# Up projections of three MLPs: high and low parts of the activations moved side by side as 512 columns

## The chip, the cores and the metric

The kernel runs on one core of one Trainium2 chip. The metric is device microseconds (us) for one execution of the whole program, from its start to its end on that core; lower is better. The median of three executions of the kernel before is 1496.93 us.

## What is computed

Two blocks of a network follow each other on the same 256 tokens of 1024 features. The first block has a short convolution layer and an RWKV layer, the second a sparse attention layer and a forgetting attention layer. After each of the four comes an MLP with a hidden width of 4096 and a squared ReLU, and only these MLPs matter here:

```python
# first_block, DEPTH = 2
h = _modulate(_rmsnorm(x, norm_g[i, 1]), sh2, sc2)
x = x + gt2[:, None, :] * (jnp.square(jax.nn.relu(h @ mlp_w1[i])) @ mlp_w2[i])
# second_block, DEPTH = 2
def sq_relu_mlp(xn, w_up, w_down):
    return jnp.square(jax.nn.relu(xn @ w_up)) @ w_down
```

`h @ mlp_w1` and `xn @ w_up` are the up projections (1024 to 4096), the others the down projections. All inputs and outputs are float32.

## The kernel before, in words

**Numbers in two parts.** Each float32 matrix is split into a high part (rounded to the type fp32r) and a low part (the rest). A product is the sum of three: high by high, high weight by low activation, low weight by high activation. The helper `three` (lines 1949 to 1951) issues these three matmuls into one accumulating PSUM bank.

**Units.** Weights arrive in units of 1 MB. SP loads a unit into one of four `stage` buffers, once the unit four before it has been split (`lo_made`). ScalarE copies it into `w_hi` (line 775) and VectorE subtracts to make `w_lo` (line 1310), each in two halves of 128 x 1024 elements. `w_hi` and `w_lo` have two buffers each, so unit u + 2 is split after unit u is done (`unit_done`) and while unit u + 1 is being multiplied.

**An MLP** has four groups, and each group has four up units and four down units; the two kinds take turns by group. An up unit multiplies eight row tiles of `h` (index `kt`) by two blocks of 128 output features (index `m`): 8 x 2 x 3 = 48 matmuls, with the weights as the stationary operand and 256 tokens as the moving one (128x256). It writes one bank, `un[0]` or `un[1]` in turn; the block `m` is one half of the bank. A down unit (`wide_unit`, lines 1990 to 1992) is 24 matmuls of 512 columns into the four `acc` banks.

**Behind an up unit**, in this order: ScalarE takes the ReLU out of PSUM (`relu_b`, line 932); VectorE forms max(un, 0) x relu into `zf` (line 1496), waits for it to be finished and then frees the bank with an `engine_nop` (`un_free`); both engines then split the weights of unit u + 2; ScalarE copies `zf` to `z_hi` (line 920) and VectorE subtracts to `z_lo` (line 1390). After the last up unit of a group (`j` = 3) the order differs: first half of the weights, then `z_hi` and `z_lo`, then the second half. `z_hi` and `z_lo` are what the down units multiply.

**Around an MLP.** `stat_ps` and `misc` are the two other PSUM banks. They serve norms, transposes and rows that are broadcast: before the MLP of the RWKV layer (`m` = 1), `row_copy(3, stat_ps, misc)` on ScalarE reads both (lines 915 and 916), after ScalarE has made the `h` tiles and split weights. Before the MLPs of the attention layers (`m` = 2, 3) the tiles of `h` are read from `acc`, `stat_ps` and `misc`. In the first unit of an MLP, TensorE waits for each tile of `h_lo` in turn, and transposes further tiles in between. In the first group of `m` = 2 and 3, the norm's sums are worked out beside the up units (`both_rms` on VectorE and `both_roots` on ScalarE, at `j` = 2).

**Names of the change:** `h_hi` and `h_lo` (SBUF, eight tiles of 256 columns each, in regions of their own), `un`, `stat_ps`, `misc`, `relu_b`, the functions `mlp` of the three engines and `unit` of TensorE.

## Time and profile before

| | us |
|---|---|
| median of three executions | 1496.93 (1493.68 to 1499.69) |
| the profiled execution, as timed | 1501.27 |
| its span in the trace | 1499.5 |
| mean granted TensorE clock | 0.969 of 2.4 GHz |

| engine | busy us | share of the span |
|---|---|---|
| TensorE, matmul | 1426.8 | 95% |
| TensorE, weight load | 1252.1 | 84% |
| VectorE | 854.6 | 57% |
| ScalarE | 696.3 | 46% |
| GpSimd | 112.5 | 8% |

The costliest groups of instructions by summed busy time (the records of matmuls overlap, so their sums are larger than the time that they take on the engine):

| line, engine | what | count | busy us | mean ns |
|---|---|---|---|---|
| L1310 VectorE | `w_lo` from `stage` and `w_hi` | 378 | 454.2 | 1239 |
| L775 ScalarE | `w_hi` from `stage` | 378 | 379.8 | 1049 |
| L1949 to L1951 TensorE | `un` from `h` and weights, 256 columns | 3 x 1536 | 449.2, 439.7, 439.5 | 292, 286, 286 |
| L1990 to L1992 TensorE | `acc` from `z` and weights, 512 columns | 3 x 640 | 252.9, 249.5, 249.3 | 395, 390, 390 |
| L932 ScalarE | `relu` from `un` | 64 | 38.2 | 597 |
| L1496 VectorE | `zf` from `un` and `relu` | 64 | 44.2 | 691 |
| L1390 VectorE | `z_lo` | 68 | 46.6 | 685 |

How to read it: a matmul's record runs from its start to its modelled end, and the next one starts before that end. What a matmul costs in a dense stream is the distance from its start to the next start. The time of an up unit is the distance between two ReLUs that each waited for TensorE. The chain of waits puts 88% of the span on TensorE.

### The profile page before, as it was taken

How to read it: one execution, taken by the hardware profiler on the slowest of the kernel's cores; microseconds unless marked ns; L12 is line 12 of the kernel's file. 1: busy time of each engine (PE TensorE's matmuls, PEld its weight loads, DVE VectorE, ACT ScalarE, POOL GpSimd, SP SyncE). 2: the span in 40 equal slices, each digit the busy share in tenths (PEclk: the TensorE clock that was granted, in tenths of full speed). 3: DMA queues.
4: the chain of work that ended last, by engine and by line, in shares of the span. 5: the costliest groups of instructions: out<-in, count | busy, mean ns of one | idle time of the engine just before them, and what ended most of it. 6: DMA issues, size and time to landing. Idle time of an engine off the chain costs nothing.

```text
span 1499.5 us, 28573 instructions
## 1 busy us (share of the span) xinstructions
PE 1426.8 (95%) x12399; PEld 1252.1 (84%) x12399; DVE 854.6 (57%) x1320; ACT 696.3 (46%) x1192; POOL 112.5 (8%) x114
## 2 busy tenths in 40 slices
PE   4999999999899999988999998899999999999997
PEld 1987778878697899868988997689999899899986
DVE  1447634446657445556555658766555668665555
ACT  2434533334376322445444534655444557564443
POOL 0000000010100444410000001100000012000000
PEclk8999999999998999989999979999999999999999
DMA  9998699945334200014566533236556454365551
GB/s 359 382 323 300 240 361 302 309 149 169 88 117 152 72 4 3 3 38 171 189 196 191 162 116 110 85 103 207 183 183 197 144 169 136 119 211 178 190 194 56
DMA packets 177430, 257.17 MB, mean 172 GB/s; under 512 B 10425, under 2 KB 122361, under 8 KB 177305
## 3 DMA queue, kind: packets, MB, share of 16 engines
q1 hardware_dynamic: 177304, 255.35, 51.3%
q8 instruction: 98, 1.61, 0.5%
q14 instruction: 28, 0.22, 0.0%
HBM read 254.28 MB, written 1.05 MB: 170 GB/s over the span
## 4 chain that ended last, share of the span: by engine, by line
PE 88%; DVE 5%; ACT 3%; DMA 1%; issue 1%; SPq 1%; POOL 0%; DVEq 0%; ACTq 0%; POOLq 0%
PE un L1949 14%; PE un L1950 14%; PE un L1951 14%; PE acc L1990 10%; PE acc L1991 9%; PE acc L1992 9%; PE acc L2248 4%; PE misc L2100 3%; DMA ada_buf<-in_ada_w 1%; DVE w_lo L1310 1%; PE misc L2248 1%; PE un L2248 1%; PE stat_ps L2248 1%; PE acc L2242 1%; ACT w_hi L775 1%
## 5 line engine op out<-in xcount | busy, mean ns | idle before, releaser
L1310 DVE TENSOR_TENSOR w_lo<-stage,w_hi 128x1024 fp32r<-128x1024 f32 (+1 forms) x378 | 454.2, 1239 | 298.8 <-ACT w_hi L775 298.1
L775 ACT ACTIVATE w_hi<-stage 128x1024 fp32r<-128x1024 f32 (+1 forms) x378 | 379.8, 1049 | 256.4 <-PE acc L1992 224.0
L1949 PE MATMUL un<-h_hi,w_hi 128*128 128x256 f32 x1536 | 449.2, 292 | 2.9 <-DVE h_lo L1368 2.8
L1950 PE MATMUL un<-h_lo,w_hi 128*128 128x256 f32 x1536 | 439.7, 286 | 0.0
L1951 PE MATMUL un<-h_hi,w_lo 128*128 128x256 f32 x1536 | 439.5, 286 | 0.0
L1949 PEld LDWEIGHTS un<-h_hi,w_hi 128*128 128x128 f32 x1536 | 300.3, 196 | 19.6 <-issue 11.1
L1950 PEld LDWEIGHTS un<-h_lo,w_hi 128*128 128x128 f32 x1536 | 300.4, 196 | 1.7 <-issue 1.2
L1951 PEld LDWEIGHTS un<-h_hi,w_lo 128*128 128x128 f32 x1536 | 299.9, 195 | 0.0
L1990 PE MATMUL acc<-w_hi,z_hi 128*128 128x512 f32 x640 | 252.9, 395 | 0.8 <-DVE pair_logit L1787 0.7
L1991 PE MATMUL acc<-w_lo,z_hi 128*128 128x512 f32 x640 | 249.5, 390 | 0.0
L1992 PE MATMUL acc<-w_hi,z_lo 128*128 128x512 f32 x640 | 249.3, 390 | 0.0
L1990 PEld LDWEIGHTS acc<-w_hi,z_hi 128*128 128x128 f32 x640 | 120.2, 188 | 31.1 <-issue 6.3
L1992 PEld LDWEIGHTS acc<-w_hi,z_lo 128*128 128x128 f32 x640 | 120.1, 188 | 25.5
L1991 PEld LDWEIGHTS acc<-w_lo,z_hi 128*128 128x128 f32 x640 | 120.3, 188 | 23.6
L932 ACT ACTIVATE relu<-un 128x512 f32<-128x512 f32 x64 | 38.2, 597 | 182.3 <-PE un L1951 182.3
L1496 DVE SCALAR_TENSOR_TENSOR zf<-un,relu 128x512 f32<-128x512 f32 x64 | 44.2, 691 | 134.2 <-ACT relu L932 134.1
L2100 PE MATMUL misc<-ada_buf,c_rep 128*32 128x256 f32 x704 | 48.8, 401 | 0.0
L1390 DVE TENSOR_TENSOR z_lo<-zf,z_hi 128x512 fp32r<-128x512 f32 x68 | 46.6, 685 | 0.0
L920 ACT ACTIVATE z_hi<-zf 128x512 fp32r<-128x512 f32 x68 | 42.3, 622 | 7.5 <-DVE zf L1583 7.5
L1949 PE MATMUL un<-z_hi,w_hi 128*128 128x256 f32 x128 | 36.9, 288 | 1.4 <-DVE w_lo L1310 0.9
L754 POOL TENSOR_TENSOR pair_bias<-const,cum_k 128x256 f32<-128x256 f32 (+1 forms) x16 | 15.8, 1011 | 293.0 <-ACT cum_k L1258 255.9
L2248 PE MATMUL acc<-inv_t,t 64*64 64x32 f32 x640 | 36.7, 219 | 0.2
(369 smaller groups left out, 1656.1 us busy)
## 6 DMA issues: line engine op xcount, KB each, us to landing
stage<-in_mlp_w SPq DMA_DIRECT2D x64, 1024.0 KB
ada_buf<-in_ada_w SPq DMA_DIRECT2D x48, 1024.0 KB, 7.5
stage<-in_w_up SPq DMA_DIRECT2D x32, 1024.0 KB
stage<-in_w_down SPq DMA_DIRECT2D x32, 1024.0 KB
stage<-in_conv_w_in SPq DMA_DIRECT2D x12, 1024.0 KB
stage<-in_rw_w_rkv SPq DMA_DIRECT2D x12, 1024.0 KB
stage<-in_w_in_a SPq DMA_DIRECT2D x8, 1024.0 KB
stage<-in_w_kv_b SPq DMA_DIRECT2D x8, 1024.0 KB
```

What stands on the lines that cost most here:

```text
L775: A_(w_hi[u % 2][:, half, 0:n], stage[u % NSTAGE][:, half, 0:n], ACT.Copy).then_inc(hi_made, 1)
L1310: V.tensor_tensor(w_lo[u % 2][:, half, 0:n], stage[u % NSTAGE][:, half, 0:n], w_hi[u % 2][:, half, 0:n].bitcast(F32), ALU.subtract).then_i ...
L1390: V.tensor_tensor(z_lo[:, 2 * j:2 * j + 2, :], zf[zc % 2][:], z_hi[:, 2 * j:2 * j + 2, :].bitcast(F32), ALU.subtract).then_inc(z_lo_made, 1)
L1496: V.scalar_tensor_tensor(out=zf[k % 2][:], in0=un[(v + j) % 2][:], scalar=0.0, in1=relu_b[j % 2][:], op0=ALU.max, op1=ALU.mult).then_inc(z ...
L1949: MM(out, hi_l, hi_r, start=start, stop=False, skip_group_check=True)
L1950: MM(out, hi_l, lo_r, start=False, stop=False, skip_group_check=True)
L1951: return MM(out, lo_l, hi_r, start=False, stop=stop, skip_group_check=True)
L1990: MM(y, z_hi[:, kt, q], wh[:, i, :], start=(first and kt == 0), stop=False, skip_group_check=True)
L1991: MM(y, z_hi[:, kt, q], wl[:, i, :], start=False, stop=False, skip_group_check=True)
L1992: ins = MM(y, z_lo[:, kt, q], wh[:, i, :], start=False, stop=(last and kt == KT - 1), skip_group_check=True)
L2100: ins = MM(ada_sums(s)[32 * j:32 * j + 32, s % 2, :], c_rep[:, 2 * q + t, :], ada_buf[ada_slot(k)][:, t, 2 * P * j:2 * P * (j + 1)], start ...
L2248: ins = MM(out_[rows], lhs[rows], rhs[rows], start=start, stop=stop, skip_group_check=True)
```

## The change

In the MLPs `m` = 1, 2 and 3 (the first MLP, `m` = 0, stays as it is):

- `h_hi` and `h_lo` become two halves of one tensor `h_both`, so that the high and the low part of a tile lie side by side, 512 columns. Everything else that uses the two names reads or writes the same data at the new addresses.
- An up unit (`up_unit`) multiplies the high weights by these 512 columns in one matmul and the low weights by the 256 high columns in a second one. High weight by high activation and low weight by high activation gather in the first half of a bank, high weight by low activation in the second half. The two output blocks need a bank each, so a unit takes a pair of banks: `un` as one pair, and `stat_ps` with `misc` as the other.
- ScalarE copies the second halves of both banks to SBUF (`up_sum`) instead of taking the ReLU; VectorE adds the first halves to them and frees the pair with that instruction; then it forms max(s, 0) x s into `zf` from SBUF alone. The `engine_nop` goes.
- TensorE waits at the start of such an MLP until both `un` banks are free, and in `m` = 1 before its second unit until `row_copy(3, ...)` is done (`row_out` at 4).

```diff
@@ -133,7 +133,10 @@
-        h_hi, h_lo, z_hi, z_lo = (at(n, FM, o, F32R) for n, o in zip(("h_hi", "h_lo", "z_hi", "z_lo"), act_off))
+
+        h_both = at("h_both", [P, KT, 2, SEQ], act_off[0], F32R)
+        h_hi, h_lo = h_both[:, :, 0, :], h_both[:, :, 1, :]
+        z_hi, z_lo = (at(n, FM, o, F32R) for n, o in zip(("z_hi", "z_lo"), act_off[2:]))
@@ -191,6 +194,7 @@
+        up_sum = [at(f"up_sum{i}", [P, 2, SEQ], scr_off + 16 * 1024 + 2048 * i) for i in range(2)]
@@ -277,9 +281,12 @@
-        un = [ctx.enter_context(nc.psum_tensor(f"un{i}", [P, 2, SEQ], F32)) for i in range(2)]
-        stat_ps = ctx.enter_context(nc.psum_tensor("stat_ps", [P, 2, SEQ], F32))
-        misc = ctx.enter_context(nc.psum_tensor("misc", [P, 2, SEQ], F32))
+        un_pair = ctx.enter_context(nc.psum_tensor("un", [P, 2, 2, SEQ], F32))
+        side_pair = ctx.enter_context(nc.psum_tensor("side", [P, 2, 2, SEQ], F32))
+        un = [un_pair[:, i, :, :] for i in range(2)]
+        stat_ps, misc = side_pair[:, 0, :, :], side_pair[:, 1, :, :]
+
+        up_pair = (un_pair, side_pair)
@@ -928,8 +936,12 @@
-                        act.wait_ge(unit_done, uu + 1)
-                        A_(relu_b[j % 2][:], un[(v + j) % 2][:], ACT.Relu).then_inc(relu_ready, 1)
+                        if m == 0:
+                            act.wait_ge(unit_done, uu + 1)
+                            A_(relu_b[j % 2][:], un[(v + j) % 2][:], ACT.Relu).then_inc(relu_ready, 1)
+                        else:
+                            act.wait_ge(unit_done, uu + 1)
+                            A_(up_sum[j % 2][:], up_pair[j % 2][:, :, 1, :], ACT.Copy).then_inc(low_copied, 1)
@@ -1492,11 +1504,18 @@
-                        dve.wait_ge(relu_ready, 4 * GROUPS * m + UPD * g + j + 1)
-                        V.scalar_tensor_tensor(out=zf[k % 2][:], in0=un[(v + j) % 2][:], scalar=0.0, in1=relu_b[j % 2][:],
-                                               op0=ALU.max, op1=ALU.mult).then_inc(zf_ready, 1)
-                        dve.wait_ge(zf_ready, zf_count(k))
-                        V.engine_nop().then_inc(un_free, 1)
+                        if m == 0:
...
+                        else:
+                            dve.wait_ge(low_copied, 4 * GROUPS * (m - 1) + UPD * g + j + 1)
+                            V.tensor_tensor(up_sum[j % 2][:], up_pair[j % 2][:, :, 0, :], up_sum[j % 2][:], ALU.add).then_inc(un_free, 1)
+                            dve.wait_ge(un_free, freed(v + UPD * g + j))
+                            V.scalar_tensor_tensor(out=zf[k % 2][:], in0=up_sum[j % 2][:], scalar=0.0, in1=up_sum[j % 2][:],
+                                                   op0=ALU.max, op1=ALU.mult).then_inc(zf_ready, 1)
@@ -1974,6 +1993,20 @@
+            def up_unit(u, pair, ready=None):
+
+                wh, wl = w_hi[u % 2], w_lo[u % 2]
+                for kt in range(KT):
+                    if kt % (KT // 2) == 0:
+                        pe.wait_ge(lo_made, 2 * u + kt // (KT // 2) + 1)
+                    if ready is not None:
+                        ready(kt)
+                    for m in range(2):
+                        c = slice(P * m, P * m + P)
+                        MM(pair[:, m, :, :], wh[:, kt, c], h_both[:, kt, :, :], start=(kt == 0), stop=False, skip_group_check=True)
+                        ins = MM(pair[:, m, 0, :], wl[:, kt, c], h_hi[:, kt, :], start=False, stop=(kt == KT - 1), skip_group_check=True)
+                ins.then_inc(unit_done, 1)
+
@@ -2121,10 +2154,19 @@
-                        free_bank(v + UPD * g + j)
-                        unit(u + 2 * UPD * g + j, un[(v + j) % 2], (h_hi, h_lo), h_ready(n) if g == 0 and j == 0 else None)
+                        ready = h_ready(n) if g == 0 and j == 0 else None
                         if m == 0:
+                            free_bank(v + UPD * g + j)
+                            unit(u + 2 * UPD * g + j, un[(v + j) % 2], (h_hi, h_lo), ready)
                             ada_piece(S_MLP + 2 * UPD * g + j)
+                        else:
+                            if g == 0 and j == 0:
+                                pe.wait_ge(un_free, freed(v - 1))
+                            else:
+                                free_bank(v + UPD * g + j)
+                            if m == 1 and g == 0 and j == 1:
+                                pe.wait_ge(row_out, 4)
+                            up_unit(u + 2 * UPD * g + j, up_pair[j % 2], ready)
```

## Rows read from the trace of the kernel before

**Rows 1.** The page, parts 1 and 2: busy us of TensorE and VectorE, granted clock.
```profile
PE 1426.8 (95%) x12399; PEld 1252.1 (84%) x12399; DVE 854.6 (57%) x1320; ACT 696.3 (46%) x1192; POOL 112.5 (8%) x114
...
PEclk8999999999998999989999979999999999999999
```

**Rows 2.** Windows: busy us of each engine, MLPs m = 1, 2, 3.
```profile
core 0: us, PE busy (x) PEld busy (x) DVE busy (x) ACT busy (x) POOL busy (x), PEclk, DMA share, GB/s
688.66:867.50 178.84, 178.84 (x1153) 163.85 (x1153) 103.71 (x112) 86.28 (x115) 0.00 (x0) 1.00 0.56 180
1006.40:1186.00 179.60, 179.57 (x1160) 164.49 (x1160) 103.63 (x117) 88.05 (x121) 0.00 (x0) 1.00 0.57 186
1310.60:1489.00 178.40, 178.37 (x1152) 163.52 (x1152) 101.04 (x112) 85.47 (x115) 0.00 (x0) 1.00 0.52 168
```

**Rows 3.** Chain of waits in one group of m = 3 (1362.5 to 1407.3).
```profile
by line: PE un L1951 17.4%; PE un L1950 17.1%; PE un L1949 17.1%; PE acc L1991 16.2%; PE acc L1992 16.2%; PE acc L1990 16.2%
```

**Rows 4.** Timeline of TensorE, up to down and back: start, us, line, operation.
```profile
1379.54 0.28 PE L1951 MATMUL un<-h_hi,w_lo 128*128 128x256 f32 x1
1379.66 0.40 PE L1990 MATMUL acc<-w_hi,z_hi 128*128 128x512 f32 x1
1379.90 0.40 PE L1991 MATMUL acc<-w_lo,z_hi 128*128 128x512 f32 x1
...
1401.22 0.39 PE L1992 MATMUL acc<-w_hi,z_lo 128*128 128x512 f32 x1
1401.45 0.28 PE L1949 MATMUL un<-h_hi,w_hi 128*128 128x256 f32 x1
1401.56 0.28 PE L1950 MATMUL un<-h_lo,w_hi 128*128 128x256 f32 x1
```

**Rows 5.** Timeline of ScalarE in m = 3; in brackets idle time and releaser.
```profile
1379.86 0.60 ACT L932 ACTIVATE relu<-un 128x512 f32<-128x512 f32 x1 [2.75 <-PE un L1951]
1407.40 0.60 ACT L932 ACTIVATE relu<-un 128x512 f32<-128x512 f32 x1 [3.69 <-PE un L1951]
1413.16 0.60 ACT L932 ACTIVATE relu<-un 128x512 f32<-128x512 f32 x1 [2.75 <-PE un L1951]
1413.66 2.00 ACT L775 ACTIVATE w_hi<-stage 128x1024 fp32r<-128x1024 f32 x2
1415.55 0.62 ACT L920 ACTIVATE z_hi<-zf 128x512 fp32r<-128x512 f32 x1
```

**Rows 6.** Timeline of VectorE behind up units of m = 3.
```profile
1413.79 0.69 DVE L1496 SCALAR_TENSOR_TENSOR zf<-un,relu 128x512 f32<-128x512 f32 x1 [1.85 <-ACT relu L932]
1414.74 2.36 DVE L1310 TENSOR_TENSOR w_lo<-stage,w_hi 128x1024 fp32r<-128x1024 f32 x2 [0.26 <-ACT w_hi L775]
1417.02 0.68 DVE L1390 TENSOR_TENSOR z_lo<-zf,z_hi 128x512 fp32r<-128x512 f32 x1
...
1428.00 1.22 DVE L1310 TENSOR_TENSOR w_lo<-stage,w_hi 128x1024 fp32r<-128x1024 f32 x1
```

**Rows 7.** Timeline of VectorE: an add of PSUM and SBUF.
```profile
1310.86 0.69 DVE L1405 TENSOR_TENSOR x<-acc,x 128x512 f32<-128x512 f32 x1
```

**Rows 8.** Timelines at j = 2 of the first group, m = 3: ScalarE, then VectorE.
```profile
1333.98 0.30 ACT L856 ACTIVATE norm_st<-norm_st,small 128x2 f32<-128x2 f32 x1 [1.69 <-DVE norm_st L1351]
...
1335.34 0.16 DVE L1511 TENSOR_TENSOR small<-norm_st 128x2 f32<-128x2 f32 x1
```

**Rows 9.** Start of m = 1: ScalarE's row copy, and TensorE's second unit.
```profile
693.83 0.59 ACT L916 ACTIVATE gate_row<-misc 128x512 f32<-128x512 f32 x1
...
693.91 0.35 PE L1949 MATMUL un<-h_hi,w_hi 128*128 128x256 f32 x1
```

**Rows 10.** Start of m = 3: VectorE's weights of the second unit, and TensorE there.
```profile
1316.12 2.36 DVE L1310 TENSOR_TENSOR w_lo<-stage,w_hi 128x1024 fp32r<-128x1024 f32 x2 [0.46 <-ACT w_hi L775]
...
1317.18 0.28 PE L1951 MATMUL un<-h_hi,w_lo 128*128 128x256 f32 x1
1317.49 0.36 PE L1949 MATMUL un<-h_hi,w_hi 128*128 128x256 f32 x1
1317.69 0.28 PE L1950 MATMUL un<-h_lo,w_hi 128*128 128x256 f32 x1
```

More of the change, by code:

```diff
@@ L643, in build @@
         silu_e, silu_ready, rep_ready = sem("silu_e"), sem("silu_ready"), sem("rep_ready")
+        low_copied = sem("low_copied")
         @block.gpsimd
@@ L1494, in mlp @@
                         k = zc + UPD * g + j
-                        dve.wait_ge(relu_ready, 4 * GROUPS * m + UPD * g + j + 1)
-                        V.scalar_tensor_tensor(out=zf[k % 2][:], in0=un[(v + j) % 2][:], scalar=0.0, in1=relu_b[j % 2][:],
-                                               op0=ALU.max, op1=ALU.mult).then_inc(zf_ready, 1)
-                        dve.wait_ge(zf_ready, zf_count(k))
-                        V.engine_nop().then_inc(un_free, 1)
+                        if m == 0:
+                            dve.wait_ge(relu_ready, UPD * g + j + 1)
+                            V.scalar_tensor_tensor(out=zf[k % 2][:], in0=un[(v + j) % 2][:], scalar=0.0, in1=relu_b[j % 2][:],
+                                                   op0=ALU.max, op1=ALU.mult).then_inc(zf_ready, 1)
+                            dve.wait_ge(zf_ready, zf_count(k))
+                            V.engine_nop().then_inc(un_free, 1)
+                        else:
[3 more added lines that the diff above has]
+                            V.scalar_tensor_tensor(out=zf[k % 2][:], in0=up_sum[j % 2][:], scalar=0.0, in1=up_sum[j % 2][:],
+                                                   op0=ALU.max, op1=ALU.mult).then_inc(zf_ready, 1)
                         if j < UPD - 1:
```

## The prediction, made before the changed kernel was run

> **What bounds the kernel now.** I read the page's busy shares first: the matmuls fill 95% of the span, VectorE 57%, ScalarE less [rows 1]. A share over the whole span mixes stages, so next came the windows of the three MLPs that the change touches. In each, TensorE is busy to within 0.03 us of the whole window, at a granted clock of 1.00, which is the 2.4 GHz level; VectorE is busy 101.04 to 103.71 us out of about 179 [rows 2]. Then the chain of waits in one whole group: its six lines are all TensorE's and add up to 100% [rows 3]. So in these 537 us (178.84 + 179.60 + 178.40) TensorE alone sets the time, and what counts is the distance between starts of matmuls. The records' lengths (0.28 and 0.40) overlap and are no cost.
>
> **TensorE's part.** Each three matmuls of 256 columns (3 x 120.0 = 360.0 ns) become one of 512 and one of 256. Taking the rows' price for each, 226.9 + 120.0 = 346.9 ns. There are 16 such in a unit: 5.76 us become 5.55 us, 0.21 us less. 48 units (3 MLPs x 16) give 10.1 us at most. The down units do not change.
>
> The rows say 13 ns of fixed cost per matmul. The Trainium skill (TensorE: Matmul & The Clock Gate, section "Back-to-back issue gap") gives N / 2.4 + 2.5 ns for N columns, 109 and 216 ns; a merge would then save 2.5 ns, and 768 merges 1.9 us in all. By that rule this change hardly pays. The trace disagrees with it on both widths (120.0 and 226.9), so the sum does not use it; it returns beside a rival.
>
> **The price of the 512 columns beside PSUM reads.** Just behind an up unit, while ScalarE starts to read `un`, a 512 took 0.24 us and not 0.227 [rows 4, 5]. In the changed units, a PSUM read runs for 0.60 (copy) + 0.69 (add) = 1.29 us out of each unit, which is about 3.7 of its 512s. I bound their surcharge by 0 and 13 ns and take the middle, 6 ns: 3.7 x 6 x 48 = 1.1 us lost (0 to 2.3). The 256s show none: one such is the 0.12 at the end of the up unit.
>
> **Starts of the MLPs.** Here the next unit does not begin when TensorE is through.
> - m = 2 and 3: the second unit begins at 1317.49, 0.31 after the last matmul of the first, because the first half of its `w_lo` (1316.12 + half of 2.36) is done only at 1317.30 [rows 10]. A shorter first unit waits longer for the same thing. Of 16 units, 15 gain: 15 x 0.21 = 3.15 us for each of the two MLPs.
> - m = 1: the second unit now takes `stat_ps` and `misc`, and so waits for the row copy that ends on ScalarE at 693.83 + 0.59 = 694.42. Today it begins at 693.91 [rows 9]. With 0.1 us to 0.2 us from the end of an operation to the waiting matmul (1317.30 to 1317.49 above), it begins at about 694.57: 0.6 us later, not 0.21 earlier. Behind that wait on TensorE's queue is everything. 15 x 0.21 - 0.6 = 2.5 us.
> - The wait on both `un` banks at the start costs nothing, since transposes, norms or down units lie between the last use of `un` and the MLP. The other pair is free for the same reason in m = 2 and 3: the tiles of `h` read from it must be made before the first unit can finish.
>
> Sum: 2.5 + 2 x 3.15 - 1.1 = 7.7 us.
>
> **VectorE's and ScalarE's part: beside the path.** ScalarE's ReLU (0.60) becomes a copy of as many elements, again from PSUM; I take 0.60. VectorE gets an add of one PSUM and one SBUF operand, for which there is a row of the same shape, 0.69 us [rows 7]. The other form, max times self, now reads SBUF alone; before it took 0.69 from PSUM and `z_lo`, all from SBUF, takes 0.68 [rows 6]; I take 0.69. With some 0.06 us for the wait on its own add, everything behind it on VectorE comes 0.75 us later: 48 x 0.75 = 36 us more VectorE, on 308 us busy in 537. Is it covered?
> - Middle units (j < 3). From the end of a unit: copy 0.60, add and product to 2.1, then `w_lo` for unit u + 2: first half at about 3.4, second at 4.5 (2.36 for both [rows 6]). TensorE needs them at 5.55 and, four tiles later, at 8.3. Slack 2.1 us for the first.
> - `z_hi` waits on ScalarE until `zf` exists: today ScalarE comes to it at 1415.55, `zf` ended at 1414.48 [rows 5, 6]. 0.75 later is 1415.23, still in time. At j = 3 `z_hi` comes one weight half earlier, so `z_hi` and the second half slip by some 0.7.
> - j = 3. The unit's copy starts at 1413.16 + 2 x 5.76 = 1424.7 [rows 5]. The second half of `w_lo` ends today at 1428.00 + 1.22 = 1429.2 [rows 6]; it will be 1430.0. TensorE needs it when the down unit before it (24 x 0.227 = 5.45 us) and six more matmuls of 512 are done: 1424.7 + 5.45 + 1.36 = 1431.5. Slack 1.5 us.
> - The tightest is the first group of m = 2 and 3, where the norm's sums follow at j = 2. They end on VectorE at 1335.34 + 0.16, just as the next ReLU (1335.04, its end 1335.64) is over [rows 8]. All comes 0.75 later and the next unit ends up to 0.4 earlier: VectorE's chain behind j = 3 slips about 0.7 us further. That eats half of the 1.5 us and leaves 0.7 or more. `both_roots` on ScalarE then also holds back the copy of the j = 3 unit, by about 0.4 us, within this.
> - SP's loads wait for `lo_made`, which comes 0.75 later, but a unit's buffer has about three units (17 us) until it is needed, and the DMA engines are at 0.52 to 0.57 of their time at 168 to 186 GB/s [rows 2].
>
> So none of this costs anything. If the cover were gone, each late microsecond of `w_lo` would be a microsecond of the end.
>
> **The numbers.** The profiled execution took 1501.27 us and its span 1499.5, both above the median of the three, 1496.93. The matmul distances that make up the sum depend on the clock and not on that difference, so I take the sum from the median: 1496.9 - 7.7 = 1489.2 us. The bounds of its terms (surcharge 0 to 2.3, m = 1 wait 0.3 to 0.9) make 1487.8 to 1490.7, and the medians of so few executions, which spread over 6 us, add some 2 to 3 us on either side: 1485 to 1493 for this case alone.
>
> **Rivals.**
> - *The width is paid each time.* The one 512 right behind 256s took 0.24 us, not 0.227 [rows 4]. In the changed kernel every 512 follows a 256. If the cause is the change of width and not the PSUM read, a pair costs up to 0.24 + 0.12 = 0.36 us: what three cost today. Then the gain is 0 to 3 us, and 0.6 + 0 is lost at m = 1: about 1496 us. Against it: a second 512 in the same place is not slower for long, and there is a PSUM read at hand to explain it. The Trainium skill's rule of 2.5 ns, cited above, would come to nearly this time. Chance 0.14.
> - *Slower: the pipeline restarts at each switch.* The first matmul of a unit that had waited needs 0.20 us to the next one, not 0.12 [rows 10]. If alternating between banks or between full bank and half bank costs this 0.08 each pair, 768 x 0.08 = 61 us come on top: 1496.9 - 7.7 + 61 = 1550 us. It decides from 0.013 us a pair. The boundaries in the rows speak against it (0.12 and 0.11 after a new bank and width). Chance 0.05. A second way to the same side is VectorE as the bound, but with 1.5 us of slack the add and the product would have to take twice their rows; 0.02, and then some 1500 to 1510 us.
> - *More gain.* If what limits a 256 at 120.0 is the weight load before it, and a load hides wholly under a 512, the pair could take (512 + 256) / 2.4 + 13 = 333 ns, which would be 768 x 27 ns = 20.7 us less, 1478 us. The load of the next high weights still has only a 256 to hide under, as now. Chance 0.05.
>
> **How the numbers follow.** The forecast has 0.74. For this kernel 0.5% (7.5 us) is about what a measurement can tell from no change, and the forecast, 7.7, lies right at it: I give 0.43 of the 0.74 to faster by over 0.5% and 0.31 to within. More gain adds 0.05 to faster; the first rival adds 0.14 to within, less 0.01 by scatter: faster 0.49, same 0.44, slower 0.07. The range takes in the first rival and leaves out the slower one and most of the larger gain: 1483 to 1497 us.
>
> **What would show it.** In the changed kernel's windows of the same MLPs: TensorE busy all the time, each about 2.5 to 3.2 us shorter. The distance from copy to copy of middle up units should be 5.55 to 5.58 us (5.76 would be the first rival, 7 the second). The starts should alternate between 0.227 and 0.12. At the second unit of m = 1 a wait on ScalarE L916's counterpart should stand. In a down stage nothing should change, 21.78 us for four units; if TensorE waits for `w_lo` there, at j = 3 or in the first group of m = 2 or 3, my VectorE sum is wrong. It would all be wrong if the granted clock in these windows fell below 1.00.

## The result, and the profile after

The changed kernel takes 1488.74 us (median of ten, 1484.57 to 1490.94) against 1496.54 us of the kernel before on the same chips: 7.8 us less. The ratio is 0.9942, with a 95% interval from 0.9927 to 0.9957. The forecast was 1489.2 us. The profiled execution took 1487.04 us, its span 1485.2 us.

The page, parts 1 and 2, answering to [rows 1] (busy us by engine; granted clock in tenths):

```profile
PE 1408.3 (95%) x11631; PEld 1200.0 (81%) x11631; DVE 887.2 (60%) x1368; ACT 698.4 (47%) x1192; POOL 115.5 (8%) x114
...
PEclk8999999999999999989999999999999999999999
```

There are 768 matmuls fewer, TensorE is as full as before, and VectorE is busy for 33 us more, where 36 were forecast.

The windows of the three MLPs, cut at the same places of the work as [rows 2]:

```profile
682.80:860.58 177.78, 177.26 (x899) 150.19 (x898) 113.38 (x128) 86.54 (x114) 0.00 (x0) 1.00 0.56 180
995.92:1173.70 177.78, 177.66 (x906) 150.72 (x906) 113.41 (x133) 88.71 (x121) 0.00 (x0) 1.00 0.60 187
1298.24:1474.78 176.54, 176.44 (x897) 149.63 (x896) 110.80 (x128) 86.07 (x115) 0.00 (x0) 1.00 0.53 170
```

They were 178.84, 179.60 and 178.40 us: 1.1, 1.8 and 1.9 us less, 4.7 us in all, where 7.7 us were forecast. TensorE still hardly waits in them: 0.5 us in m = 1 and 0.1 us in each of the others. So each unit saves less than forecast, and the timeline of ScalarE shows it, in the group that answers to [rows 5]:

```profile
1349.55 0.60 ACT L944 ACTIVATE up_sum<-un 128x512 f32<-128x512 f32 x1 [3.57 <-PE un L2007]
1355.20 0.60 ACT L944 ACTIVATE up_sum<-side 128x512 f32<-128x512 f32 x1 [2.63 <-PE side L2007]
...
1366.51 0.60 ACT L944 ACTIVATE up_sum<-side 128x512 f32<-128x512 f32 x1 [2.63 <-PE side L2007]
```

(1366.51 - 1349.55) / 3 = 5.65 us a unit, not 5.55. The matmuls of one such unit, and of one in the first group of m = 3 (timeline of TensorE: start, length, line):

```profile
1361.01 0.40 PE L2006 MATMUL side<-h_both,w_hi 128*128 128x512 f32 x1
1361.24 0.28 PE L2007 MATMUL side<-h_both,w_lo 128*128 128x256 f32 x1
...
1362.07 0.40 PE L2006 MATMUL side<-h_both,w_hi 128*128 128x512 f32 x1
```

```profile
1316.02 0.40 PE L2006 MATMUL un<-h_both,w_hi 128*128 128x512 f32 x1
...
1317.07 0.39 PE L2006 MATMUL side<-h_both,w_hi 128*128 128x512 f32 x1
```

Three pairs take 1.06 us in the one, 353 ns a pair, and 1.05 us in the other. Over whole units the difference is plain: from copy to copy 5.65 or 5.66 us in nearly all, 5.55 to 5.59 in the second and third unit behind the first copy of m = 2 and 3, where 5.55 was forecast for all.

**Where the other 9.5 us of the two profiled spans come from.** Cut at the copies that stand behind the first and the last up unit of each MLP, the spans of four traces, two of each kernel, compare like this (us):

| stretch | before | before_again | after | after_again |
|---|---|---|---|---|
| start to the last up unit of m = 0 | 350.53 | 348.07 | 348.18 | 348.50 |
| RWKV layer | 343.77 | 340.59 | 340.21 | 341.23 |
| up units of m = 1, first to last | 151.60 | 151.60 | 150.59 | 150.30 |
| sparse attention layer | 166.77 | 166.77 | 163.23 | 163.17 |
| m = 2 | 151.99 | 152.00 | 150.17 | 150.14 |
| forgetting attention layer | 152.83 | 152.82 | 152.77 | 152.66 |
| m = 3 | 152.00 | 152.00 | 150.15 | 150.20 |

The first two rows vary from trace to trace of one kernel; they are chance, and make the single spans differ by more than the medians. But the row of the sparse attention layer is 3.6 us shorter each time. It begins with the last four down units of m = 1 and ends with the first up unit of m = 2, which is 0.11 us shorter by the merge (6.72 us from its first matmul to its copy, 6.83 before); the rest of the work is the same in both kernels. Its windows, from the last ReLU or copy of m = 1 to the first of m = 2, and the first low-clock stretch in each, a stretch at a granted clock of 0.50 (the last three columns are granted clock, DMA share and GB/s); the kernel before, then the changed one:

```profile
845.90:1012.68 166.78, 155.75 (x1001) 131.51 (x999) 118.09 (x230) 88.86 (x201) 11.04 (x8) 0.93 0.35 110
873.30:890.40 17.10, 17.10 (x82) 17.10 (x81) 9.22 (x24) 5.08 (x13) 0.00 (x0) 0.50 0.20 62
```

```profile
838.98:1002.20 163.22, 152.19 (x984) 126.71 (x982) 118.61 (x231) 89.00 (x200) 10.91 (x8) 0.95 0.36 112
...
871.20:878.00 6.80, 6.80 (x33) 6.80 (x33) 4.21 (x15) 2.78 (x5) 0.00 (x0) 0.50 0.45 146
```

At a granted clock of 0.50, the 1.2 GHz level, TensorE was busy all of those 17.1 and 6.8 us. Each window has two more such stretches. In all, 23.9 us are at the 1.2 GHz level in both traces of the kernel before, and 17.1 us in both of the changed one: 6.8 us fewer. At half the clock these would cost 3.4 us, by estimate, which is about what the row differs by. What TensorE did before the clock fell, in the kernel before (timeline of TensorE):

```profile
870.80 1.09 PE L2052 MATMUL acc<-const,xs_sq 128*128 128x128 f32 x8 [0.81 <-DVE xs_sq L1444]
872.98 0.39 PE L1949 MATMUL un<-h_hi,w_hi 128*128 128x256 f32 x1 [1.09 <-DVE h_lo L1368]
```

Between the MLP and the attention layer it waits twice, 0.81 and 1.09 us, with eight short transposes between; the changed kernel waits there 0.81 and 1.08 us. So two things stand to be explained: 5.65 us a unit instead of 5.55, and 3.6 us in a layer that the change hardly touches.

### The profile page after: what moved, and what is told of

Same layout as the page of the kernel before. It is cut to its first block, busy times and chain, and to the rows that moved or that the text cites. A ratio compares the mean times of both kernels' runs of the same rounds, so it can differ in the third digit from the quotient of the medians.

```text
span 1485.2 us, 27037 instructions
## 1 busy us (share of the span) xinstructions
PE 1408.3 (95%) x11631; PEld 1200.0 (81%) x11631; DVE 887.2 (60%) x1368; ACT 698.4 (47%) x1192; POOL 115.5 (8%) x114
## 3 DMA queue, kind: packets, MB, share of 16 engines
HBM read 254.28 MB, written 1.05 MB: 172 GB/s over the span
## 4 chain that ended last, share of the span: by engine, by line
PE 87%; DVE 5%; ACT 3%; issue 1%; DMA 1%; SPq 1%; POOL 0%; DVEq 0%; ACTq 0%; POOLq 0%
PE acc L2023 10%; PE acc L2024 9%; PE acc L2025 9%; PE un L1968 8%; PE un L1970 7%; PE un L1969 7%; PE side L2006 6%; PE un L2006 6%; PE acc L2290 4%; PE side L2007 3%; PE un L2007 3%; PE side L2133 3%; PE side L2290 2%; DMA ada_buf<-in_ada_w 1%; DVE w_lo L1322 1%
## 5 line engine op out<-in xcount | busy, mean ns | idle before, releaser
L1968 PE MATMUL un<-h_both,w_hi 128*128 128x256 f32 x768 | 227.1, 296 | 3.0 <-DVE h_both L1380 2.8
L1969 PE MATMUL un<-h_both,w_hi 128*128 128x256 f32 x768 | 218.9, 285 | 0.0
L1970 PE MATMUL un<-h_both,w_lo 128*128 128x256 f32 x768 | 218.8, 285 | 0.0
L1968 PEld LDWEIGHTS un<-h_both,w_hi 128*128 128x128 f32 x768 | 149.0, 194 | 18.4 <-issue 10.1
L1969 PEld LDWEIGHTS un<-h_both,w_hi 128*128 128x128 f32 x768 | 149.1, 194 | 1.3 <-issue 1.2
L1970 PEld LDWEIGHTS un<-h_both,w_lo 128*128 128x128 f32 x768 | 148.9, 194 | 0.0
L2006 PE MATMUL un<-h_both,w_hi 128*128 128x512 f32 x384 | 138.4, 402 | 0.0
L2006 PE MATMUL side<-h_both,w_hi 128*128 128x512 f32 x384 | 136.5, 398 | 0.7 <-ACT gate_row L924 0.5
L2007 PE MATMUL un<-h_both,w_lo 128*128 128x256 f32 x384 | 108.2, 282 | 0.0
L2007 PE MATMUL side<-h_both,w_lo 128*128 128x256 f32 x384 | 107.6, 280 | 0.0
L2006 PEld LDWEIGHTS side<-h_both,w_hi 128*128 128x128 f32 x384 | 72.1, 188 | 19.3 <-issue 1.6
L2006 PEld LDWEIGHTS un<-h_both,w_hi 128*128 128x128 f32 x384 | 72.8, 190 | 17.8 <-issue 0.4
L2007 PEld LDWEIGHTS un<-h_both,w_lo 128*128 128x128 f32 x384 | 73.1, 190 | 0.4
L2007 PEld LDWEIGHTS side<-h_both,w_lo 128*128 128x128 f32 x384 | 72.5, 189 | 0.0
```

What stands on the lines that cost most here:

```text
L1968: MM(out, hi_l, hi_r, start=start, stop=False, skip_group_check=True)
L1969: MM(out, hi_l, lo_r, start=False, stop=False, skip_group_check=True)
L1970: return MM(out, lo_l, hi_r, start=False, stop=stop, skip_group_check=True)
L2006: MM(pair[:, m, :, :], wh[:, kt, c], h_both[:, kt, :, :], start=(kt == 0), stop=False, skip_group_check=True)
L2007: ins = MM(pair[:, m, 0, :], wl[:, kt, c], h_hi[:, kt, :], start=False, stop=(kt == KT - 1), skip_group_check=True)
```

## Experiments

### A second trace of both kernels

Nothing edited. The question is what the low clock does from run to run.

> The kernel before, unchanged, for a second trace. In the first traces the stretch between the first copy of the RWKV layer's MLP and the last copy of each MLP became 4.7 us shorter in all by the change (1.0, 1.8 and 1.9 us), but the span became 14.2 us shorter; 7.1 us of the rest lie in two stretches that the change does not touch, the RWKV layer and the sparse attention layer, 3.56 us each. The granted clock of before shows two stretches of 17.1 us at half rate there, that of after shows 6.8 us in the same places. Theory A (chance): where the low-clock stretches fall and how long they last differs from run to run of the same kernel; then this trace has another set of them than the first one of before, and its MLP stretches are as before, 151.60, 151.99 and 152.00 us. Theory B (the change itself spares them): this trace shows both 17.1 us stretches again.

> The changed kernel, unchanged, for a second trace. Theory A (low-clock stretches fall by chance): MLP stretches again 150.59, 150.17 and 150.14 us, and the low-clock stretches elsewhere are others than in the first trace; ratio to before 0.994. Theory B (the change spares them): again 6.8 us in both places and nowhere 17.1 us outside the start of the kernel.

Measured: before_again 1495.58 us; after_again 1488.98 us, ratio 0.9954 (0.9934 to 0.9974). The MLP stretches came again to within 0.3 us (table above). The low-clock stretches followed neither theory throughout: in the RWKV layer they came in other places and lengths, as theory A has it (one that lasted 17.1 us in the first trace of before lasted 10.2 us in the second); in the sparse attention layer both traces of a kernel agree with each other, as theory B has it.

### Undoing only the merge: three_narrow

```diff
-                        MM(pair[:, m, :, :], wh[:, kt, c], h_both[:, kt, :, :], start=(kt == 0), stop=False, skip_group_check=True)
+                        MM(pair[:, m, 0, :], wh[:, kt, c], h_hi[:, kt, :], start=(kt == 0), stop=False, skip_group_check=True)
+                        MM(pair[:, m, 1, :], wh[:, kt, c], h_lo[:, kt, :], start=False, stop=False, skip_group_check=True)
```

> Undoes only the merge: bank pairs, ScalarE's copy, VectorE's add and all waits stay as in the changed kernel, but each pair of matmuls is again three of 256 columns (low activations into the second half of the bank). Theory (the merge is the only gain and all that is added is covered): 5.76 us from copy to copy of an up unit, as before, no wait of TensorE for weights, and 0.6 us lost at the second unit of m = 1, so 1497 us, ratio 1.000. Rival (the added add and the later un_free cost something that the merge has hidden): more than 5.76 us a unit or waits on w_lo, and a ratio of 1.001 or more. Rival (writing two banks in turn costs time): distance of starts above 120 ns at each change of bank, 5.8 to 5.9 us a unit.

Measured: 1496.98 us, ratio 1.0001 (0.9984 to 1.0019). Timeline of ScalarE in m = 3:

```profile
1358.27 0.60 ACT L944 ACTIVATE up_sum<-un 128x512 f32<-128x512 f32 x1 [3.69 <-PE un L2008]
1364.03 0.60 ACT L944 ACTIVATE up_sum<-side 128x512 f32<-128x512 f32 x1 [2.75 <-PE side L2008]
```

5.76 us a unit, as before, and m = 1 is 0.6 us longer (152.22 against 151.60 us from first to last copy). In the MLPs, all that was added beside the merge costs these 0.6 us and nothing else; two banks in turn cost nothing at 256 columns. The layers between the MLPs took other times in this trace (164.70 us in the sparse attention layer instead of 166.77), which is taken up below.

### Fewer changes of width: wide_first and two_and_two

wide_first:

```diff
                         MM(pair[:, m, :, :], wh[:, kt, c], h_both[:, kt, :, :], start=(kt == 0), stop=False, skip_group_check=True)
+                for kt in range(KT):
+                    for m in range(2):
+                        c = slice(P * m, P * m + P)
                         ins = MM(pair[:, m, 0, :], wl[:, kt, c], h_hi[:, kt, :], start=False, stop=(kt == KT - 1), skip_group_check=True)
```

> The changed kernel with another order in an up unit: first the 16 matmuls of 512 columns, then the 16 of 256. In the changed kernel a pair takes 353.4 ns in nearly all units (233 to 241 from a 512 to the next start, 113 to 120 from a 256), where 226.9 + 120.0 = 346.9 was forecast, so that a unit takes 5.655 us and not 5.55. Theory W (each change of width costs some 3 ns): there is one change of width in a unit and not 31, the unit takes 5.55 to 5.57 us, 48 units save 4 to 5 us more: 1484 us, ratio 0.991. Rival P (the PSUM reads of ScalarE and VectorE slow the 512s): only the 512s that run beside the copy and the add are above 227; nearly all of these reads now fall on 512s, 1.3 us of them in each unit, and the unit takes 5.57 to 5.60 us; the slow ones stand at the unit's start alone. Rival B (the change of bank costs it): two banks still take turns at each matmul, so the unit stays near 5.65 us, ratio 0.994.

Measured: 1483.23 us, ratio 0.9928 (0.9904 to 0.9952). Timeline of TensorE in m = 3, with like matmuls merged into one row (start of the first, time to the end of the last, count):

```profile
1344.05 2.08 PE L2010 MATMUL un<-h_both,w_lo 128*128 128x256 f32 x16
1345.96 3.82 PE L2006 MATMUL side<-h_both,w_hi 128*128 128x512 f32 x16
1349.62 0.64 PE L2010 MATMUL side<-h_both,w_lo 128*128 128x256 f32 x4
```

16 of 256 in 1.91 us, 119 ns each; 16 of 512 in 3.66 us, 229 ns each, 2 ns above the 226.9 of a down unit. Together 5.57 us a unit, at the upper end of what theory W said and the lower end of rival P, and 148.8 us from first to last copy of each MLP instead of 150.2. Rival B falls, since here the bank changes at each matmul. Rival P is left by this run, but the trace of the changed kernel settles it. In the unit that begins at 1361.01 the add that reads PSUM is over at 1361.49 + 0.69 = 1362.18, and later three pairs still take 1.06 us, as they did beside the reads:

```profile
1361.49 0.69 DVE L1515 TENSOR_TENSOR up_sum<-un,up_sum 128x512 f32<-128x512 f32 x1 [1.37 <-ACT up_sum L944]
```

```profile
1364.19 0.40 PE L2006 MATMUL side<-h_both,w_hi 128*128 128x512 f32 x1
...
1365.25 0.40 PE L2006 MATMUL side<-h_both,w_hi 128*128 128x512 f32 x1
```

A stretch of the kernel before says the same: VectorE reads `acc` for 1.29 us beside a stream of 512s, and three of them take 0.68 us, 0.227 each.

```profile
1306.99 1.29 DVE L1405 TENSOR_TENSOR x<-acc,x 128x512 f32<-128x512 f32 x2 [4.35 <-PE acc L1992]
```

```profile
1307.02 0.39 PE L1991 MATMUL acc<-w_lo,z_hi 128*128 128x512 f32 x1
...
1307.70 0.39 PE L1991 MATMUL acc<-w_lo,z_hi 128*128 128x512 f32 x1
```

two_and_two:

```diff
                         MM(pair[:, m, :, :], wh[:, kt, c], h_both[:, kt, :, :], start=(kt == 0), stop=False, skip_group_check=True)
+                    for m in range(2):
+                        c = slice(P * m, P * m + P)
                         ins = MM(pair[:, m, 0, :], wl[:, kt, c], h_hi[:, kt, :], start=False, stop=(kt == KT - 1), skip_group_check=True)
```

> The changed kernel, with the four matmuls of a row tile in the order 512, 512, 256, 256, so a unit has 15 changes from 256 to 512 and 16 from 512 to 256 instead of 31 in all (counting both ways: 16 instead of 32). In the traces so far a 512 takes 226.9 ns behind other 512s, 233 to 241 behind a 256, and a 256 behind a 512 takes 113 to 120. Theory W (the first 512s behind a 256 pay about 9 ns, the first 256 behind a 512 gets 3 to 7 back): half as many changes, half of the 0.10 us above 5.55: 5.60 us a unit. Rival B (it is the change of bank): here the bank changes at each matmul, 32 times instead of 16, and the unit takes more than 5.655 us, about 5.75.

Measured: 1484.16 us in one execution. Timeline of TensorE:

```profile
1345.34 0.63 PE L2006 MATMUL un<-h_both,w_hi 128*128 128x512 f32 x2
1345.80 0.39 PE L2009 MATMUL un<-h_both,w_lo 128*128 128x256 f32 x2
1346.03 0.63 PE L2006 MATMUL un<-h_both,w_hi 128*128 128x512 f32 x2
```

The unit takes 5.57 us, as with a single change: 0.46 us for two of 512 and 0.23 for two of 256. I had expected half of the surcharge to stay (5.60). So the price is not so much for each change of width. It is paid in strict alternation, and two in a row are enough to lose nearly all of it.

### Fewer changes of bank: bank_by_bank

```diff
-                for kt in range(KT):
+                for kts, ms in (((kt,), (0, 1)) for kt in range(KT)) if ready is not None else ((range(KT), (0,)), (range(KT), (1,))):
...
-                    for m in range(2):
+                        for m in ms:
```

> The changed kernel, with the 16 matmuls of one output block (one bank) first and then those of the other, except in each MLP's first unit: one change of bank inside a unit instead of 15, and the same alternation of 512 and 256. Theory W (width): 5.655 us a unit, as in the changed kernel. Rival B (bank): 5.55 us.

Measured: 1484.35 us in one execution; in m = 3, timeline of ScalarE:

```profile
1346.90 0.60 ACT L944 ACTIVATE up_sum<-un 128x512 f32<-128x512 f32 x1 [3.57 <-PE un L2008]
1352.55 0.60 ACT L944 ACTIVATE up_sum<-side 128x512 f32<-128x512 f32 x1 [2.64 <-PE side L2008]
1358.21 0.60 ACT L944 ACTIVATE up_sum<-un 128x512 f32<-128x512 f32 x1 [2.65 <-PE un L2008]
```

Still 5.65 us. The change of bank is out; every kernel tried here with units of 5.65 us alternates 512 and 256 strictly, and none of the others does. The single execution is shorter than the changed kernel's median by its other stretches (the RWKV layer took 337.40 us in it), not by its units.

### Does the end of the MLP decide what the low clock costs?

before_longer (and, the same kernel, before_longer_again):

```diff
+                    if m == 1 and g == GROUPS - 1:
+                        free_bank(v + UPD * GROUPS)
+                        for _ in range(17):
+                            MM(un[v % 2][:, 0, :], h_hi[:, 0, 0:P], h_hi[:, 1, :], start=True, stop=True, skip_group_check=True)
                     if g == GROUPS - 1:
```

> The kernel before, with 17 matmuls of 256 columns of work that nobody uses ahead of the last four down units of the RWKV layer's MLP (m = 1): 17 x 0.12 = 2.04 us more of TensorE. From the last ReLU of that MLP to the first of the next took 166.77 us in both traces of before and 163.2 in both of the changed kernel, with a low-clock stretch of 17.1 us beginning 27.4 us after that ReLU in the one and of 6.8 us beginning 32.2 us after it in the other. Theory S (the length of this MLP decides where the low clock falls in the attention layer behind it; the changed kernel's MLP is 1.0 to 1.3 us shorter, and that is what saves 3.6 us there): with the end moved by 2.0 us the low stretches come as in the changed kernel, and from ReLU to ReLU it takes 163.2 + 2.0 = 165.3 us, less than the 166.77 without the extra work. Rival C (chance, or something that the changed instructions do): 166.77 + 2.04 = 168.8 us.

> The kernel before with 17 matmuls more ahead of the last four down units of m = 1, once more. Theory S: again 165.4 us from the last ReLU of that MLP to the first of m = 2, as in its first trace, against 166.77 in both of before. Rival C: another value, 168.8 most of all.

after_longer is the changed kernel with 11 such matmuls in the same place:

> The changed kernel, with 11 matmuls of 256 columns (1.32 us) that nobody uses ahead of the last four down units of m = 1, so that this MLP ends again as late after its start as before the change (150.3 + 1.3 = 151.6 us). Theory S (the end of that MLP decides what the low clock costs in the attention layer): from its last copy to the first of m = 2 it takes 166.8 + 1.3 = 168.1 us, with a low-clock stretch of 17.1 us in it, 4.9 us more than the 163.2 of the changed kernel, for 1.3 us of work. Rival C (what saves there is the changed instructions, or chance): 163.2 + 1.3 = 164.5 us.

Windows of before_longer, before_longer_again and after_longer, from the last ReLU or copy of m = 1 to the first of m = 2:

```profile
840.64:1006.01 165.37, 154.43 (x1017) 129.80 (x1016) 118.04 (x230) 88.70 (x200) 10.92 (x8) 0.95 0.35 110
```

```profile
846.08:1011.46 165.38, 154.40 (x1018) 129.74 (x1016) 118.07 (x230) 88.73 (x200) 10.92 (x8) 0.95 0.35 111
```

```profile
839.01:1006.99 167.98, 156.94 (x995) 131.84 (x993) 118.64 (x231) 88.99 (x200) 11.02 (x8) 0.93 0.36 109
```

All three came out as theory S had them, within 0.15 us. 2.04 us of work that nobody uses make the stretch of the kernel before 1.4 us shorter (165.4 instead of 166.77) and lift its mean granted clock from 0.93 to 0.95. 1.32 us in the changed kernel make it 4.8 us longer (167.98 instead of 163.2), and the clock is at 0.93 again. So the 3.6 us are not in the changed instructions: a shift of the layer in time, and nothing else, turns either kernel's time there, less the added work, into the other's (165.4 - 2.0 = 163.4 and 168.0 - 1.3 = 166.7 us). In the changed kernel the MLP that is 1.0 to 1.3 us shorter makes the shift, and the time at the 1.2 GHz level behind it is 17.1 us in all instead of 23.9. How the chip comes to either is not shown.

### How far that rule goes: two_and_two_timed and wide_first_longer

The first is two_and_two unchanged; the second is wide_first with five matmuls that nobody uses, in the same place as above.

> The order 512, 512, 256, 256 again, timed. Its first trace had 5.57 us a unit, 149.3 us from first to last copy of each MLP, and 160.66 us (not 166.77) from the MLP m = 1 to m = 2. Against before that is 2.2 + 2.7 + 2.7 = 7.6 us in the MLPs and 6.1 us in the attention layer: 13.7 us less, ratio 0.991, if the low-clock stretches of the attention layer again follow the length of the MLP ahead of it (theory S: 160.66 again, within 0.1). If they fall by chance (rival C), another value stands there and the ratio is near 0.993 to 0.995.

> The order with all 512s first, and 5 matmuls of 256 columns more (0.6 us) that nobody uses, ahead of the last four down units of m = 1. Without them this kernel took 165.32 us from that MLP to the next, where the order 512, 512, 256, 256, whose MLP m = 1 is 0.55 us longer, took 160.66. Theory S (the end of the MLP decides): with 0.6 us more in front, the low-clock stretches come as in two_and_two and the stretch takes some 161.1 us, 4.2 us less than without the extra work; the median is 1 to 3 us under that of two_and_two or equal to it. Rival C (chance): 165.3 + 0.6 = 165.9 us.

Windows of the same stretch, two_and_two, two_and_two_timed, wide_first and wide_first_longer:

```profile
840.55:1001.21 160.66, 149.63 (x984) 124.61 (x982) 118.42 (x231) 88.84 (x201) 10.90 (x8) 0.97 0.37 114
```

```profile
839.58:1003.05 163.47, 152.43 (x984) 127.07 (x982) 119.71 (x231) 89.00 (x200) 10.92 (x8) 0.95 0.36 112
```

```profile
834.57:999.89 165.32, 154.00 (x985) 128.46 (x985) 120.47 (x231) 89.04 (x200) 10.92 (x8) 0.94 0.36 112
```

```profile
838.02:1002.94 164.92, 153.53 (x990) 127.72 (x989) 120.64 (x231) 88.99 (x200) 10.92 (x8) 0.95 0.37 112
```

Both expectations missed: 163.47 us, not 160.66, and 164.92, not 161.1. The same kernel can give either of two values here, so the end of the MLP does not decide alone. Two traces of other experiments say so too. In three_narrow and two_more_adds (below) the last down unit of m = 1 ends 0.6 and 0.5 us later behind the first copy than in the kernel before, at nearly the same point, and the windows are:

```profile
843.01:1007.71 164.70, 153.75 (x1000) 129.38 (x999) 119.61 (x231) 89.04 (x200) 10.91 (x8) 0.94 0.36 111
```

```profile
843.34:1005.46 162.12, 151.08 (x984) 125.64 (x982) 120.82 (x235) 88.83 (x201) 10.93 (x8) 0.96 0.37 113
```

So theory S is held up only for what it was formed on, the step from before to after and back, and it is not shown that each timed execution of the changed kernel saves these 3.6 us. As for time, two_and_two_timed took 1483.23 us, ratio 0.9914 (0.9896 to 0.9932), and wide_first_longer 1485.92 us, 0.9928 (0.9905 to 0.9952). Both orders with less alternation, two_and_two and wide_first, have medians of 1483.23 us, 5.5 us under the changed kernel's and 13 to 14 us under the kernel before's. The interval of either order still overlaps that of the changed kernel (0.9927 to 0.9957); that they are better rests on the traces as much, where each MLP is 0.9 to 1.8 us shorter from first to last copy. For wide_first that says too much, since its first unit is some 0.75 us longer. From the first matmul of m = 2 to its last copy, the changed kernel, two_and_two and wide_first take:

```profile
995.48:1152.37 156.89, 156.77 (x810) 133.40 (x810) 99.92 (x116) 77.56 (x104) 0.00 (x0) 1.00 0.60 188
```

```profile
994.53:1150.48 155.95, 155.81 (x810) 133.05 (x810) 99.86 (x116) 77.51 (x103) 0.00 (x0) 1.00 0.60 189
```

```profile
992.42:1148.68 156.26, 155.88 (x810) 133.59 (x810) 99.87 (x116) 77.43 (x104) 0.00 (x0) 1.00 0.59 189
```

That is 0.9 and 0.6 us less than the changed kernel, so in m = 2 two_and_two is 0.3 us ahead. The medians decide nothing between the two orders.

### How much cover VectorE's work has: two_more_adds

```diff
                             V.scalar_tensor_tensor(out=zf[k % 2][:], in0=up_sum[j % 2][:], scalar=0.0, in1=up_sum[j % 2][:],
                                                    op0=ALU.max, op1=ALU.mult).then_inc(zf_ready, 1)
+                            dve.wait_ge(zf_ready, zf_count(k))
+                            for _ in range(2):
+                                link(V.tensor_tensor(up_sum[j % 2][:], zf[k % 2][:], zf[k % 2][:], ALU.add))
```

> The changed kernel with two more adds of 128x512 elements on VectorE behind each product, which nobody uses: 2 x 0.75 = 1.5 us later for all that follows on VectorE, 48 times, 72 us in all. Theory (VectorE's work beside the up units is covered, with 1.5 us of slack at j = 3 and some 0.7 in the first group of m = 2 and 3): in middle units and groups nothing changes, 5.655 us from copy to copy and 27.43 across a down stage; TensorE waits for w_lo in the first groups of m = 2 and 3 only, 1 us each: about 2 us in all. Rival (VectorE is already at its limit): each added microsecond appears, up to 70 us more.

Measured: 1499.24 us in one execution. From first to last copy, m = 1, 2, 3 took 151.67, 154.96 and 153.53 us, against 150.30, 150.14 and 150.20 in after_again: 9.5 us more, for 96 adds of 0.69 us on VectorE. In the first group of m = 3 (timelines of ScalarE and of TensorE):

```profile
1325.19 0.60 ACT L944 ACTIVATE up_sum<-un 128x512 f32<-128x512 f32 x1 [1.41 <-PE un L2010]
1332.60 0.58 ACT L944 ACTIVATE up_sum<-side 128x512 f32<-128x512 f32 x1
```

```profile
1337.83 0.50 PE L2026 MATMUL acc<-w_hi,z_hi 128*128 128x512 f32 x1 [1.53 <-DVE w_lo L1322]
```

The middle units keep 5.65 us, so the rival is wrong. But the expected 2 us was too little by far: in this first group the copy behind j = 3 now waits for ScalarE's norm roots (7.41 us from copy to copy), which wait for VectorE's sums, and `w_lo` then comes 1.53 us late. Each later stretch across a down stage takes 27.85 us instead of 27.43. There, in the last group of m = 3 (copy at 1422.26, timeline of VectorE, then of TensorE):

```profile
1427.89 3.49 DVE L1322 TENSOR_TENSOR w_lo<-stage,w_hi 128x1024 fp32r<-128x1024 f32 x3
```

```profile
1428.71 0.40 PE L2028 MATMUL acc<-w_hi,z_lo 128*128 128x512 f32 x1
1429.17 0.51 PE L2026 MATMUL acc<-w_hi,z_hi 128*128 128x512 f32 x1
```

The second half of `w_lo` is the first of these three instructions and ends at about 1429.1, 6.85 us behind the copy, where it was 4.94 in the changed kernel. That is 1.9 us later and not 1.5, because VectorE's work for one unit now takes a little longer than 5.65 us and falls 0.12 us further behind at each (the first add starts 0.63 us behind the copy at j = 0 and 1.00 us at j = 3). TensorE waits for it at 1429.17, and 0.4 us are lost. 1.9 added less 0.4 lost is a slack of 1.5 us at j = 3, as forecast; what the expectation left out is that the added work piles up from unit to unit.

## Why the prediction came out right, and where it did not

The number was right, and so was the direction, but partly by two errors of opposite sign. 7.7 us were forecast in the MLPs; 4.7 to 5.0 us are there. Some 3.6 us came in a layer for which the prediction had no term. That the two together came within half a microsecond of the forecast is luck.

- **The bound.** TensorE fills the windows of the MLPs before and after, at a clock of 1.00. Right, and the reason why so small a change can be seen at all.
- **The price of the pair.** The failed step is "Taking the rows' price for each, 226.9 + 120.0 = 346.9 ns". Both prices were read from streams of one width, and added. In alternation the pair takes 353 ns in nearly all units: a unit saves 0.105 us, not 0.21. That is 4.7 us less over the 45 units that were to gain. The row of the 512 that took 0.24 us behind 256s was there [rows 4], and it was put down to the PSUM read beside it, at 1.1 us in all. No such price of PSUM reads is seen: the pairs take as long away from them. wide_first, two_and_two and bank_by_bank show that the missing gain goes with the alternation.
- **The first rival** came nearest to this mechanism, as a price at each change of width, and expected it to take back nearly the whole gain. It took half.
- **The second rival** (0.08 us at each switch) did not occur, and three_narrow shows that banks in turn are free. Nor did the third, with a pair of 333 ns.
- **The start of m = 1.** Forecast: the second unit begins 0.6 us later than before, by the row copy. In the trace:

```profile
687.91 0.59 ACT L924 ACTIVATE gate_row<-side 128x512 f32<-128x512 f32 x1
```

```profile
688.60 0.47 PE L2006 MATMUL side<-h_both,w_hi 128*128 128x512 f32 x1 [0.52 <-ACT gate_row L924]
```

  It waits 0.52 us, and three_narrow measured the whole as 0.6 us. In m = 2 and 3 the gain of the first unit is lost, as forecast.
- **VectorE.** The add takes the 0.69 us of [rows 7], the product from SBUF 0.69:

```profile
1411.53 0.69 DVE L1515 TENSOR_TENSOR up_sum<-side,up_sum 128x512 f32<-128x512 f32 x1 [1.35 <-ACT up_sum L944]
1412.25 0.69 DVE L1517 SCALAR_TENSOR_TENSOR zf<-up_sum 128x512 f32<-128x512 f32 x1
...
1414.60 1.23 DVE L1322 TENSOR_TENSOR w_lo<-stage,w_hi 128x1024 fp32r<-128x1024 f32 x1
```

  The second half of `w_lo` at j = 3 ends 4.9 us after the copy's start (1415.83 - 1410.89) where it was 4.5 before; 5.3 were forecast. It came out less late because part of the add fell into time in which VectorE had waited for `w_hi`. In the first group of m = 3 it ends 5.35 us after the copy, 0.4 us later still, where 0.7 were forecast. It was covered, as said, and the slack of 1.5 us left at j = 3 is borne out by two_more_adds.
- **The clock.** The prediction asked only whether it would stay at 1.00 in the MLPs. It did. That a shift in time of an MLP can change how long the low clock lasts in the layer behind it was not thought of.

## What to carry to other kernels

Price a matmul from a stream that has the same neighbours as the changed code will have: 227 and 120 ns, each measured among its like, gave 353 and not 347 ns in most of a strictly alternating stream, and issuing them in twos or all of one width first gave nearly all of it back. Where an engine is full without a gap, 13 ns per matmul saved are worth having, if all that is added elsewhere is shown to be covered. And before a difference of 0.2% is explained by the change, cut the span into stretches that it touches and stretches that it does not: here almost half of the gain in the traces was in the latter, and it is not sure to come again.

## What the runs showed of the hardware

- Matmuls in strict turns of 512 and 256 columns, each with weights of its own, take 353 ns a pair in nearly all units; in turns of two and two 348 (5.57 us for 16 pairs), and the same with 16 and 16.
- The same alternating stream can also run at 347 ns a pair: in the first group of an MLP, behind a stall of TensorE, two units took 5.55 to 5.59 us each, until the next down stage. But the same units took 5.65 and 5.66 us in m = 1 of the first trace of the changed kernel (in its second trace 5.55) and in m = 3 of bank_by_bank. So alternation alone does not set the pace. What decides between the two stays open; no run here was made to tell.
- Reads of PSUM by ScalarE and VectorE from other banks cost the matmuls nothing that shows: three pairs take 1.06 us beside them and 1.06 us away from them.
- Behind a full MLP and the same two waits of about 1 us, with short transposes between them, the layer that followed spent 23.9 us at the 1.2 GHz level in the kernel before, 17.1 us in the changed one and 10.2 us in two_and_two, whose second trace had 17.1 us. In the changed kernel, 1.3 us of work ahead of them made the stretch 4.8 us longer.
